# One core, two transformer blocks in split float32: lower weights last in each unit, and the order of some waits

## The reference

```
first_block:  x = even_layer(x); x = odd_layer(x); x = rms_norm(x, final_norm)
 even_layer: z = rms_norm(x) @ w_in (1024 x 8208); 16 heads of forgetting attention (gate fa, cumulated),
             16 heads of dilated attention; y * silu(g) @ w_out (2048 x 1024), added to x
 odd_layer:  z = rms_norm(x) @ w_in (1024 x 6144); rotated q, k; retention, 4 heads of 256 / 512;
             head group norm, * silu(g), @ w_out (2048 x 1024), added to x
second_block: u, q, k, v = rms_norm(h) @ w_in (1024 x 1280)
 y_ssm  = s5_mixer(u): complex state space over 2048 states, gelu, @ w_glu, gate
 y_attn = sliding-window attention with sinks, 8 query heads, 2 kv heads, rotary on 16 of 64 channels
 h += rms_norm(concat(rms_norm(y_ssm), rms_norm(y_attn)) @ w_out)
 h += rms_norm(silu(gate) * up @ w_down),  gate and up = rms_norm(h) @ w_gate_up, d_ff 2816
```

## Time and profile before

| | us |
|---|---|
| median of 3 executions | 814.52 (814.52 to 817.28) |
| profiled execution | 815.45, its span 813.6 |
| TensorE busy | 783.8 (96%) |
| VectorE busy | 525.3 (65%) |
| ScalarE busy | 403.6 (50%) |
| GpSimd busy | 218.1 (27%) |
| DMA | 130.70 MB, 161 GB/s mean |

### The profile page before, as it was taken

How to read it: one execution, slowest core, us unless ns; L and a number is a source line. 1 busy time by engine, 2 the same in 40 slices (tenths; PEclk the granted TensorE clock), 3 DMA queues, 4 the chain that set the end, 5 groups by cost and what they waited for, 6 DMA issues and landing times.

```text
span 813.6 us, 12652 instructions
## 1 busy us (share of the span) xinstructions
PE 783.8 (96%) x5115; PEld 683.6 (84%) x5115; DVE 525.3 (65%) x767; ACT 403.6 (50%) x640; POOL 218.1 (27%) x180
## 2 busy tenths in 40 slices
PE   8899999899999999999999999998998999999997
PEld 7689998899878889997778888888777888888885
DVE  4656864775558556875557965775668667677553
ACT  5644436434455444344335544616756655555451
POOL 3022893290621000027009910143002110111010
PEclk9999999999999999999999999998998999999999
DMA  9797992577712464644545555520363665655651
GB/s 225 181 242 219 224 202 99 119 170 179 160 50 78 163 198 129 213 156 153 162 148 152 183 193 174 185 74 2 103 211 122 186 205 182 182 177 188 206 181 52
DMA packets 77820, 130.70 MB, mean 161 GB/s; under 512 B 4414, under 2 KB 28210, under 8 KB 77634
## 3 DMA queue, kind: packets, MB, share of 16 engines
q1 hardware_dynamic: 76418, 125.00, 52.9%
q0 software_dynamic: 1200, 4.83, 2.1%
q10 hardware_dynamic: 144, 0.07, 0.0%
HBM read 128.82 MB, written 1.06 MB: 160 GB/s over the span
## 4 chain that ended last, share of the span: by engine, by line
PE 89%; DVE 5%; DMA 2%; issue 2%; ACT 1%; POOL 0%; SPq 0%; DVEq 0%; POOLq 0%; ACTq 0%
PE ps L1462 41%; PE ps L1479 17%; PE ps L1492 10%; PE ps L1493 5%; DMA stage<-in_even_w_in 2%; PE ps L1556 2%; PE ps L1575 2%; PE ps L1586 1%; PE ps L1588 1%; PE ps L1587 1%; PE ps L1855 1%; PE ps L1739 1%; DVE w_lo L871 1%; PE ps L1819 1%; PE ps L1683 1%
## 5 line engine op out<-in xcount | busy, mean ns | idle before, releaser
L871 DVE TENSOR_TENSOR w_lo<-stage,w_hi 128x1024 fp32r<-128x1024 f32 x232 | 303.3, 1325 | 168.6 <-ACT w_hi L596 168.1
L596 ACT ACTIVATE w_hi<-stage 128x1024 fp32r<-128x1024 f32 x232 | 242.8, 1061 | 247.5 <-PE ps L1462 121.0
L1462 PE MATMUL ps<-w_hi,act_t 128*128 128x512 f32 (+1 forms) x688 | 221.9, 392 | 8.4 <-DVE w_lo L871 5.9
L1462 PEld LDWEIGHTS ps<-w_hi,act_t 128*128 128x128 f32 x688 | 129.0, 189 | 36.2 <-issue 6.6
L1479 PE MATMUL ps<-act_t,w_hi 128*128 128x256 f32 x832 | 151.9, 284 | 0.0
L1462 PE MATMUL ps<-w_lo,act_t 128*128 128x512 f32 (+1 forms) x376 | 145.3, 387 | 0.0
L1479 PEld LDWEIGHTS ps<-act_t,w_hi 128*128 128x128 f32 x832 | 130.8, 193 | 0.3 <-DVE w_lo L871 0.2
L1492 PE MATMUL ps<-act_t,w_hi 128*128 128x512 f32 x352 | 126.0, 402 | 0.3 <-DVE act_t L908 0.3
L1479 PE MATMUL ps<-act_t,w_lo 128*128 128x256 f32 x416 | 117.6, 283 | 0.0
L1493 PE MATMUL ps<-act_t,w_lo 128*128 128x256 f32 x352 | 99.5, 283 | 0.0
L1462 PEld LDWEIGHTS ps<-w_lo,act_t 128*128 128x128 f32 x376 | 71.1, 189 | 14.5 <-issue 1.0
(11 more groups left out here) (356 smaller groups left out, 1114.1 us busy)
## 6 DMA issues: line engine op xcount, KB each, us to landing
stage<-in_even_w_in SPq DMA_DIRECT2D x64, 512.0 KB, 5.2
stage<-in_odd_w_in SPq DMA_DIRECT2D x48, 512.0 KB, 4.2
stage<-in_w_gate_up SPq DMA_DIRECT2D x44, 512.0 KB, 4.5
stage<-in_w_down SPq DMA_DIRECT2D x22, 512.0 KB, 4.0
stage<-in_even_w_out SPq DMA_DIRECT2D x16, 512.0 KB, 4.2
stage<-in_odd_w_out SPq DMA_DIRECT2D x16, 512.0 KB, 4.2
stage<-in_w_in SPq DMA_DIRECT2D x10, 512.0 KB, 3.7
stage<-in_w_out SPq DMA_DIRECT2D x8, 512.0 KB, 4.7
```

What stands on the lines that cost most here:

```text
L596: nc.scalar.activation(w_hi[:, u % RING, :], stage[:, u % RING, :], ACT.Copy).then_inc(hi_ready, 1)
L871: nc.vector.tensor_tensor(w_lo[:, u % RING, :], stage[:, u % RING, :], w_hi[:, u % RING, :].bitcast(F32), ALU.subtract).then_inc(lo_ready, 1)
L1462: ins = mm(out[:, b, :], left, right, start=(k == 0 and n == 0), stop=(k == k_tiles - 1 and n == 2))
```

## The change

Units start on the upper half and come to the lower one last; the forget weights are loaded and split later; two splits of the start move; in the 16-head attentions ScalarE copies heads 0, 2, 6 and 10 (`copied_by_act`, which is also true for all heads of the sink attention), with a semaphore of its own; in the state space the splits go behind the drain of u and drives ahead of scans; k is written twice by the drain of skv; q and k are transposed and copied in three parts; nine matmuls of ones go ahead of the transposes of the updated x. `channels_unit` and the last mixing chunk are reordered as `tokens_unit` is; the last three units of down keep their order. The headings between @@ are no lines of the files.

```diff
@@ constants @@
-SPLIT_HEADS = (6, 11, 16)
+SPLIT_HEADS = (4, 8, 12)
+COPIED_BY_ACT = (0, 2, 6, 10)
...
-PARAMS_AT = 12
+FORGET_AT, PARAMS_AT = 5, 12
@@ GpSimd: DMA of the forget weights, now after the two memsets @@
-pool.wait_ge(landed[1], 16)
+pool.wait_ge(unit_used, FORGET_AT)
 pool.dma_start(wf[:, 0:KD * FOX_H].rearrange("p (k h) -> p k h", k=KD), w_even[:, :, even_at["fa"]:even_at["fa"] + FOX_H]).then_inc(wf_in, 16)
@@ ScalarE, start @@
 squares(0, lambda b: x[:, b, :], lambda b: junk[:, b, :])
-split_hi(6)
+split_hi(5)
...
 nc.scalar.activation(sp["mag"][:], sp["mdt"][:], ACT.Exp).then_inc(mag_ready, 1)
+split_hi(6)
 act.wait_ge(ang_ready, 1)
...
-act.wait_ge(wf_in, 16)
-act.wait_ge(fills, 1)
-nc.scalar.activation(wf_hi[:], wf[:], ACT.Copy).then_inc(wf_hi_ready, 1)
...
         ins.then_inc(drain_sem((kind, c)), 1)
+        if (kind, c) == ("gb", 0):
+            act.wait_ge(wf_in, 16)
+            act.wait_ge(fills, 1)
+            nc.scalar.activation(wf_hi[:], wf[:], ACT.Copy).then_inc(wf_hi_ready, 1)
@@ ScalarE, attentions @@
+def copy_prob_act(n):
+    act.wait_ge(prob_turned, n + 1)
+    if n >= 2:
+        act.wait_ge(pv_done, n - 1)
+    nc.scalar.activation(prob_t[:, n % 2, :], bank(2 + n % 2, 384), ACT.Copy).then_inc(prob_copied_act, 1)
...
         exponentials(n)
+        if copied_by_act(n - 2):
+            copy_prob_act(n - 2)
@@ ScalarE, drain of skv, copies of q and k @@
-    ins = nc.scalar.activation(qkv[:, b, SINK_H:12, :], result(("skv", 0), 256)[:, b, :].rearrange("p (h d) -> p h d", d=HD), ACT.Copy,
-                               scale=rstd_in[:, b:b + 1])
+    nc.scalar.activation(qkv[:, b, K_AT:V_AT, :].rearrange("p (k r) d -> p k r d", r=2), heads[:, 0:KV_H, :].unsqueeze(2).to_broadcast([P, KV_H, 2, HD]),
+                         ACT.Copy, scale=rstd_in[:, b:b + 1])
+    ins = nc.scalar.activation(qkv[:, b, V_AT:V_AT + KV_H, :], heads[:, KV_H:2 * KV_H, :], ACT.Copy, scale=rstd_in[:, b:b + 1])
...
-for b in range(NB):
-    nc.scalar.activation(k_twice[:, b], qkv[:, b, SINK_H:SINK_H + KV_H, :].unsqueeze(2).to_broadcast([P, KV_H, 2, HD]), ACT.Copy).then_inc(k_twice_ready, 1)
 act.wait_ge(qk_turned, 1)
-nc.scalar.activation(q_t[:].rearrange("p (a m) n -> p a (m n)", a=2), ps[:, 2 * BANK:4 * BANK].rearrange("p (a n) -> p a n", a=2), ACT.Copy)
+nc.scalar.activation(q_t[:, 0:2, :].rearrange("p m n -> p (m n)"), bank(2), ACT.Copy)
 act.wait_ge(qk_turned, 2)
 nc.scalar.activation(k_t[:], bank(1).rearrange("p (k n) -> p k n", k=2), ACT.Copy).then_inc(qk_ready, 1)
+act.wait_ge(qk_turned, 3)
+nc.scalar.activation(q_t[:, 2:4, :].rearrange("p m n -> p (m n)"), bank(3), ACT.Copy).then_inc(qk_ready, 1)
@@ VectorE, start @@
 spread(rstd[:, 0:2])
+split_lo(5)
...
 ahead(("ga", 0))
-dve.wait_ge(wf_hi_ready, 1)
-TT(wf_lo[:], wf[:], wf_hi[:].bitcast(F32), ALU.subtract).then_inc(wf_lo_ready, 1)
 take_row(0)
 for c in range(1, 4):
     ahead((("ga", "ga", "gb", "gb")[c], c % 2))
+dve.wait_ge(wf_hi_ready, 1)
+TT(wf_lo[:], wf[:], wf_hi[:].bitcast(F32), ALU.subtract).then_inc(wf_lo_ready, 1)
@@ VectorE, attentions @@
-        if 2 <= i < 18:
+        if 2 <= i < 18 and not copied_by_act(n - 2):
             copy_prob(n - 2)
@@ VectorE, state space @@
 spread(rstd_in)
-ahead(("u", 0))
...
 ins.then_inc(drain_sem(("u", 0)), 1)
+ahead(("u", 0))
...
-for ct in range(CT - 1):
-    ssm_drive(ct)
-    if ct == 1:
-        split_lo(last_unit[("skv", 0)] + 1)
-    ssm_scan(ct)
-ssm_drive(CT - 1)
+ssm_drive(0)
+ssm_scan(0)
+ssm_drive(1)
+split_lo(last_unit[("skv", 0)] + 1)
+ssm_drive(2)
+ssm_drive(3)
 chunk_drained(dve, ("sq", 0))
 chunk_drained(dve, ("skv", 0))
 rope()
-ssm_scan(CT - 1)
+ssm_scan(1)
 for i in range(8 + 3):
     if i < 8:
         score_max(32 + i, 2)
+    if i in (1, 2):
+        ssm_scan(i + 1)
@@ TensorE, units @@
-    pe.wait_ge(lo_ready, u + 1)
+    pe.wait_ge(hi_ready, u + 1)
...
+def lower_there(name, j):
+    pe.wait_ge(lo_ready, chunks[name][0] + j + 1)
...
 def tokens_unit(...)
-        for b in range(NB):
-            tok = slice(b * P, (b + 1) * P)
-            passes = ((a_hi(k)[:, tok], hi[:, i, :]), (a_hi(k)[:, tok], lo[:, i, :]), (a_lo(k)[:, tok], hi[:, i, :]))
-            for n, (left, right) in enumerate(passes):
-                ins = mm(out[:, b, :], left, right, start=(k == 0 and n == 0), stop=(k == k_tiles - 1 and n == 2))
+    for i, k in enumerate(ks):
+        there[0](k)
+        for b in range(NB):
+            mm(out[:, b, :], a_hi(k)[:, tok[b]], hi[:, i, :], start=(k == 0), stop=False)
+    for i, k in enumerate(ks):
+        there[1](k)
+        for b in range(NB):
+            mm(out[:, b, :], a_lo(k)[:, tok[b]], hi[:, i, :], start=False, stop=False)
+    lower_there(name, j)
+    for i, k in enumerate(ks):
+        for b in range(NB):
+            ins = mm(out[:, b, :], a_hi(k)[:, tok[b]], lo[:, i, :], start=False, stop=(k == k_tiles - 1))
...
 def ffn_unit(...)
+    for i, k in enumerate(ks):
+        there[1](k)
+        for m in range(2):
+            mm(out[m], hi[:, i, w[m]], both[:, :, k, :], start=(k == 0), stop=(k == KD - 1), skip_group_check=True)
+    lower_there(name, j)
+    for i, k in enumerate(ks):
+        for m in range(2):
+            ins = mm(out[m][:, 0, :], lo[:, i, w[m]], act_t[:, k, :], start=False, stop=(k == KD - 1), skip_group_check=True)
@@ TensorE, waits for activations @@
-    return lambda k: pe.wait_ge(act_lo, count + k + 1)
+    return lambda k: pe.wait_ge(act_hi, count + k + 1), lambda k: pe.wait_ge(act_lo, count + k + 1)
@@ TensorE, q and k @@
-for m in range(4):
+for m in range(2):
     for b in range(NB):
+        ins = q_pair(m, b)
 ins.then_inc(qk_turned, 1)
-pe.wait_ge(k_twice_ready, 2)
 for m in range(KV_H):
     for b in range(NB):
+        ins = nc.tensor.transpose(bank(1, P, m * S + b * P), heads_of(b, K_AT + 2 * m), ident[:])
 ins.then_inc(qk_turned, 1)
-chunk_drained(pe, ("skv", 0))
+for m in range(2, 4):
+    for b in range(NB):
+        ins = q_pair(m, b)
+ins.then_inc(qk_turned, 1)
 pe.wait_ge(qk_ready, 1)
...
+    if part == 1 and i == 0:
+        pe.wait_ge(qk_ready, 2)
@@ TensorE, transposes of the updated x @@
 for b in range(NB):
+    keep_busy((6, 3)[b], (7, 0)[b])
     for k in range(KD):
```

More of the change, by code:

```diff
@@ L317, in build, with copied_by_act, wait_copied @@
         SPLIT = (1, 2, 6, 8)
+        def copied_by_act(n):
+            return n >= FOX_H + DIL_H or n % 16 in COPIED_BY_ACT
+        def wait_copied(eng, n):
+            done = sum(copied_by_act(i) == copied_by_act(n) for i in range(n + 1))
+            eng.wait_ge(prob_copied_act if copied_by_act(n) else prob_copied, done)
         def squared_count(i):
@@ L1463, in tokens_unit, with channels_unit @@
                 ins.then_inc(unit_used, 1)
-            def channels_unit(name, j, k_tiles, columns, before=None):
+            def channels_unit(name, j, k_tiles, columns, there=always):
                 hi, lo = unit_of(name, j)
-                out = result(name)
-                for i in range(2):
-                    k = 2 * j + i
-                    if before is not None:
-                        before(k)
-                    for m in range(4):
-                        o = out[:, m // 2, (m % 2) * S:(m % 2 + 1) * S]
-                        passes = ((columns(hi[:, i, :], m), act_t[:, k, :]), (columns(lo[:, i, :], m), act_t[:, k, :]),
-                                  (columns(hi[:, i, :], m), act_t[:, KD + k, :]))
-                        for n, (left, right) in enumerate(passes):
-                            ins = mm(o, left, right, start=(k == 0 and n == 0 and m % 2 == 0), stop=(k == k_tiles - 1 and n == 2), skip_group_check=True)
+                out = [result(name)[:, m // 2, (m % 2) * S:(m % 2 + 1) * S] for m in range(4)]
+                ks = range(2 * j, 2 * j + 2)
+                for i, k in enumerate(ks):
+                    there[0](k)
+                    for m in range(4):
+                        mm(out[m], columns(hi[:, i, :], m), act_t[:, k, :], start=(k == 0 and m % 2 == 0), stop=False, skip_group_check=True)
+                for i, k in enumerate(ks):
+                    there[1](k)
+                    for m in range(4):
+                        mm(out[m], columns(hi[:, i, :], m), act_t[:, KD + k, :], start=False, stop=False, skip_group_check=True)
+                lower_there(name, j)
+                for i, k in enumerate(ks):
+                    for m in range(4):
+                        ins = mm(out[m], columns(lo[:, i, :], m), act_t[:, k, :], start=False, stop=(k == k_tiles - 1), skip_group_check=True)
@@ L1791, in _, with mix_part @@
             turn_rows(lambda b, k: y_attn[:, b, k * P:(k + 1) * P], 4, 0)
-            def mix_part(kind, c, at, before=None):
+            def mix_part(kind, c, at, there=always):
                 start_chunk((kind, c))
                 for j in range(2):
-                    tokens_unit((kind, c), j, lambda k: x_hi(at + k), lambda k: x_lo(at + k), CT, before)
```

(16 more changed lines are left out.)

84 lines of the change are left out of this document (40 added, 44 removed).

## The result

The changed kernel took 806.16 us (median of 4 executions, 803.58 to 807.22) against 814.52 (812.37 to 817.28): ratio 0.9885, 95% interval 0.9846 to 0.9924, so 8.4 us faster. Run once more later, it took 809.27 (12 executions, 802.65 to 815.02) beside 813.62 (17), ratio 0.9935 (0.9896 to 0.9975). Two of the twelve were in the chip's slower state; the ratios leave such executions out, and without the two the median is 807.92. The forecast was 801, its range 795 to 808: both times lie in its upper part, the second at its very end. The profiled execution is the fastest of its four: 803.58 us, span 801.8, 11.9 us less than the profiled one of before.

A forecast was written before the change was run, and what follows sets the result against it. TensorE, busy 783.8 of 813.6 us, was taken as the bound, through gaps, half clock and matmul pace. Terms 5.6 + 2.0 + 1.3 - 1.6 + 4.8 + 2.1 = 14.2 off 815.45, less 0.9 for the median: about 801 us, range 795 to 808.

The forecast's parts named there:

- part 1: Start, units 0 to 8 and forget weights: removed wait, earlier unit 0 and fuller clock gain 5.6 us, between 3.5 and 6.5.
- part 5: Nine matmuls of ones by the transposes of x hold the clock: 2.1 us gained, or 0.6 lost if it falls.
- parts 3 and 4: Two 16-head attentions, head copies on ScalarE: 1.6 us lost in all; state space and sink attention: 4.8 us gained.
- units 6 and 7: At the start: queues of ScalarE and VectorE make upper half 7 0.2 us late and lower half 7 0.5 us late.
- Part 2: Lower weights last, after the start: 2.0 us from the gaps before the mixing products, 1.3 from the feed-forward units.
- I leave it as it is: First 16-head attention: its one half-clock stretch, 1.6 us, was assumed to stay, so no gain was counted.
- 2.35, 2.4 and 1.2: State space: last-drive wait gone, 2.35 us; lag matmuls at full clock, up to 2.4; scans among the minima lose 1.2.
- rival B: Clock falls elsewhere, after new gaps in the attentions and before rope, and the ones don't hold it: 809 us; chance 0.17.
- A: Rival: the attentions gain all 5.9 us of gaps and their clock stretch, 1.6: 792 us; chance 0.12.
- D: Rival: matmul pace depends on order; runs changing PSUM bank each matmul cost 6 ns more on 3608 matmuls: 822; chance 0.03.
- C: Rival: only the start and mixing waits come off, 7.6 us, other removed stalls uncovering rope or a scan: 807; chance 0.08.

The follow-up runs named there:

- experiment 3: The changed kernel without the nine matmuls of ones ahead of the transposes of the updated x; 808.4 us, ratio 0.9942.
- experiment 4: The changed kernel with scans 1 and 2 back between the drives and scan 3 behind rope; 809.23 us, ratio 0.9926.
- 6: The changed kernel with the forget weights' lower half computed early and both 16-head attentions as before the change; 798.79 us, ratio 0.9805.
- Experiment 5: The changed kernel with the forget weights' lower half computed ahead of lower halves 15 to 18, not behind them; 802.88 us, ratio 0.9865.
- 7: The changed kernel with early forget weights, ScalarE copying heads 2, 6, 10 but not 0, splits at 4, 8, 12; 799.75 us, ratio 0.981.
- 8: The changed kernel with early forget weights, no head copies on ScalarE in the 16-head attentions, splits at heads 4, 8, 12; 799.64 us, ratio 0.9815.
- 9: Over 6: VectorE's last scan one step later, and five matmuls of ones ahead of unit 0; 800.12 us, ratio 0.9863.
- experiment 11: Over 6: VectorE's two splits of u's chunk back ahead of the row of scales; one execution, 801.22 us.
- 12: Over 6: VectorE's last scan one step later, behind the minima of head 35, without ones at the start; 797.88 us, ratio 0.9791.
- experiment 1: The changed kernel with the order of a unit's matmuls as before, the whole unit waiting for its lower half; 805.68 us, ratio 0.9892.
- experiment 2: The changed kernel with both 16-head attentions as before: no head copies on ScalarE, splits at heads 6, 11, 16; 802.07 us, ratio 0.9851.
- 10: The changed kernel itself run again, nothing edited; 809.27 us over all twelve executions, 807.92 without the two in the slower state.

## Why the forecast was right, and where its steps were off

The direction, the order of size and most mechanisms were right; the sum was 2.3 us too large for the profiled execution (14.2 against 11.9) and 5.1 for the medians (13.5 against 8.4). That the profiled sum is so near is in part luck: part 1 fell short by 3.4 us and part 5 by 0.9, while parts 3 and 4 came out 1.4 and 0.7 better. The second occasion's 807.92 is at the very end of the range.

**Part 1, the start, was off.** The 3.55 us went, and nothing waits for w_lo. Unit 8 started at 35.06, where the sign of being right was near 33. Three terms failed. "Unit 0 can start when upper half 0 is there (9.8)": it was 11.21, because ScalarE got its weights at 10.06 and not at 8.70; in experiments 3, 4 and 6 it was 9.6 to 9.9, so the term was right and the landing varies (8.4 to 10.1 in the fourteen profiles). "At 27.4 the clock fell ... without the gap I take it as gone": it went there and fell at 11.1 for 3.4 us instead:

```profile
11.07:14.48 3.41, 3.27 (x8) 2.62 (x9) 3.33 (x5) 3.41 (x9) 0.00 (x0) 0.50 0.82 236
```

And "The forget weights' lower half now stands behind lower half 18, which ends when TensorE finishes unit 15: 0.25 us" is the step that failed: it took the lower half 18 to follow TensorE, by slot, where in fact it follows the DMA. In the profiled execution these are 1.4, 1.7 and 1.1 us (1.38 for 0.25); the 0.7 that I had charged for units 6 and 7 did not come. I had priced late landings at "1 to 2 us" for units 9 and 10, and not looked at the one wait that another consumer had on later ones. The trace of before had a sign of it: "a landing has 8 us before anybody waits", but unit 14, issued at 38.76, landed at 47.35, and ScalarE had stood 1.48 us for it. The wait for the forget weights measured 1.4, 3.2, 3.9, 3.9 and 4.9 us in five of six profiles with that order, and the clock fell beside the last four. Experiment 5 takes it out alone. In the seven profiles with that one step moved (5 to 9, 11, 12) unit 16 starts at 56.9 to 59.8, so part 1 is worth 3.7 to 6.6 us, 4.7 in the mean, near the 5.6 of the forecast.

**Part 2** was right in both terms: 1.8 for 2.0, 1.5 for 1.3, undone in experiment 1. Two feed-forward units took 5.59 us, not 5.55. That "the order frees nothing there" (from unit 5 on) missed the 0.44 us behind the second attention.

**Part 3** was right in sign and in its gaps (1.35, 0.8, 0.8, 0.8 + 0.3 forecast; 1.24, 0.69, 0.69, 0.93 found), and by experiment 2 the copies cost 2.2 us over both halves: nearer the raw estimate of 1.0 a half than to the 1.6 I took. "I leave it as it is" failed for the clock: the half-clock stretch in the first attention was gone, worth 1.55 (31.51 us from first scores to the next projection before, 29.96 in experiment 2). So the row's -0.2 is -2.2 for the copies and splits, +1.55 for the clock by chance, and +0.44 for the order. The two attentions of before, the first with 3.4 us at half clock in its 35:

```profile
130.00:165.00 35.00, 32.01 (x253) 28.61 (x250) 25.27 (x89) 18.86 (x68) 7.32 (x7) 0.95 0.33 77
...
230.00:262.00 32.00, 28.90 (x236) 25.30 (x236) 23.47 (x89) 18.62 (x69) 3.81 (x2) 1.00 0.14 51
```

The stretch belongs to neither arrangement: with the old one it came in one of six profiles, with ScalarE's four copies in one of six too (experiment 3).

**Part 4** was right: 5.5 for 4.8. Scores of head 32 at 549.5 against "near 548", with part 1's 3.4 us missing; rope ends last with a gap of 1.02 (0.9 forecast). The parts: u 1.2 (experiment 11); drives first 3.6 net, its clock included (experiment 4), which is 4.9 less the wait of 1.25 that the scans among the minima cost, where I had 2.35, 2.4 and 1.2; one place later they cost nothing (12). The 0.7 that is left is for the copies of k and q, which no experiment undid. In the changed kernel one form of VectorE's drive step took 0.41 us with GpSimd idle and 1.51 beside it. The Trainium skill ("SBUF — State Buffer", "SBUF: two separate sides") says that the pair of ports that the two engines share is an exclusive lock for a whole instruction; the trace agrees by those 1.1 us. Of the order's worth the two scans are 4.0 us (1.80 and 2.18 in experiment 4) of VectorE's time ahead of the last read, and one such step, 1.51 in experiment 4 and 0.42 in the changed kernel, another 1.1.

```profile
531.96 0.41 DVE L1240 TENSOR_TENSOR ssm_a<-ssm_a,ssm_b 128x256 f32<-128x256 f32 x1
...
535.26 1.51 DVE L1240 TENSOR_TENSOR ssm_a<-ssm_a,ssm_b 128x256 f32<-128x256 f32 x1
```

**Part 5** was mis-sized: 1.2 for 2.1 from before to after, 0.8 by experiment 3. The clock held through the transposes with three ones between, so rival B did not strike there. The clock fell without the ones in experiment 3 and held with them in the changed kernel and the eleven other runs. The Trainium skill ("TensorE: Matmul & The Clock Gate", Part 4) holds that transposes don't count as busy in the same way: the trace doesn't contradict it, but doesn't show it either, since the ones fill gaps too. Against the gain, the first unit's wait for lower activations grew from 0.26 to 0.66 (0.26 again in experiment 3).

**Rivals.** A and D are excluded (attentions; pace 0.13 us per chunk better, not worse). C is excluded in the profile, though its 807 is near the medians: the state space gave 5.5 us, and the start and the mixing gaps 4.0, not 7.6. B, "the clock falls elsewhere", came true in part, at places that it had not named: at the start in the profiled execution (1.7 us), and beside the long waits of the forget projection in experiments 2, 3, 4 and 10. For the medians' 3.5 us this and the wait itself are the likely cause, shown in the profiles only.

## What to carry to other kernels

When a small piece of work is moved behind a queue of others, ask for each item ahead of it which resource it waits for, the slot or the transfer: the one that is late may be an item nobody needs yet. A gain upstream of a transfer-bound point is given back at the first wait on it, and shows only when that wait is moved. A helper engine that takes a copy from a busy one serves it only behind its own queue: draw the two queues for one period, as in part 3, before moving it. And take two profiles of a kernel whose executions spread by more than the question: here the first one showed the decisive wait at 1.4 us, and four others had it at 3.2 to 4.9.
